# Cached pages loaded with two neighbouring tokens to a partition, in a hybrid decoder step on one Trainium2 core

## What is computed

```python
D_MODEL = 1024; SEQ = 512; DEC_BATCH = 8; DEC_SEQ = 4; PAST_LEN = 4096; PAGE_SIZE = 128
N_HEADS = 8; HEAD_DIM = 64; MOBA_BLOCK = 256; MOBA_TOPK = 3; D_FF = 4096

def moba_sample(q, k, v, cache_k, cache_v, layer, page_table, rel_bias):
    past = cache_k[layer, page_table[:, :own * ppb]]            # 32 pages of 128 tokens for each sequence
    kmean = jnp.mean(past.reshape(DB, own, MOBA_BLOCK, N_HEADS, HEAD_DIM), axis=2)
    gate = jnp.einsum('bhtd,bhnd->bhtn', qh, kmean)             # a score for each block of two pages
    _, sel = lax.top_k(gate, n_sel)                             # the three best blocks of 16
    ...
    return moba_attend(qh, qpos, rel_bias, k_own, v_own, kpos_own, sel_part)

def layer_out(x, attn, pool, mods, w_out, norm_mlp, w_up, w_down):
    x = x + g1 * (jnp.concatenate([attn, pool], axis=-1) @ w_out)
    h = rms_norm(x, norm_mlp) * (1 + sc2) + sh2
    return x + g2 * (jnp.square(jax.nn.relu(h @ w_up)) @ w_down)
```

## Time and profile before

| | us |
|---|---|
| three runs | 883.03, 884.61, 887.43 |
| median | 884.61 |
| the profiled execution | 884.93 |
| its span, first to last instruction | 883.1 |
| TensorE busy in the span | 836.8 (95%) |
| VectorE, ScalarE, GpSimd busy | 444.8, 336.5, 292.9 |
| DMA packets | 168097, 254.03 MB |
| share of the 16 DMA engines, SyncE's queue | 83.4% |

### The profile page before, as it was taken

One profiled execution on the slowest core, in us unless ns is written; L12 is line 12 of the kernel. 1 busy time (PEld: TensorE's weight loads), 2 busy tenths in 40 slices (PEclk: granted clock), 3 DMA queues, 4 the chain that ended last, 5 costly groups with the idle time before them and its releaser, 6 DMA issues.

```text
span 883.1 us, 20264 instructions
## 1 busy us (share of the span) xinstructions
PE 836.8 (95%) x7664; PEld 590.1 (67%) x7664; DVE 444.8 (50%) x850; ACT 336.5 (38%) x701; POOL 292.9 (33%) x191
## 2 busy tenths in 40 slices
PE   5899999998998799999999999999999999999985
PEld 3677777665776366666666666667667666578874
DVE  2743222764778784664674574575565450221222
ACT  4232222887012664337127127127127127123111
POOL 0330002957132263344244244244244244323200
PEclk9799999999999899999999999999999999999998
DMA  8942226698998679999999999999899989988997
GB/s 298 335 158 96 96 74 256 197 339 258 310 305 250 221 224 313 333 346 339 319 322 309 315 320 313 303 324 316 294 340 330 343 251 365 304 315 300 396 398 281
DMA packets 168097, 254.03 MB, mean 288 GB/s; under 512 B 10502, under 2 KB 69723, under 8 KB 168027
## 3 DMA queue, kind: packets, MB, share of 16 engines
q1 hardware_dynamic: 167267, 250.66, 83.4%
q0 software_dynamic: 768, 2.51, 0.7%
HBM read 248.56 MB, written 4.75 MB: 287 GB/s over the span
## 4 chain that ended last, share of the span: by engine, by line
PE 83%; DVE 6%; DMA 3%; ACT 3%; issue 2%; POOL 1%; SPq 1%; DVEq 0%; ACTq 0%
PE PS L1587 80%; POOL hT_split L656 1%; DMA W<-in_cache_v_dram 1%; DMA mixT<-in_x_prompt_dram 1%; PE PS L1936 1%; DMA W<-in_w_up_dram 1%; PE PS L1810 1%; DVE W L1356 1%; DVE mixT L1296 1%; DVE hT L1135 1%; ACT mixT L905 1%; DVE xT L1424 1%; PE PS L2166 1%; DVE mixT L1293 0%; DVE stat L1298 0%
## 5 line engine op out<-in xcount | busy, mean ns | idle before, releaser
L718 POOL TENSOR_TENSOR W_split<-W,W_split 128x1024 fp32r<-128x1024 f32 x72 | 172.4, 2394 | 311.7 <-ACT W_split L878 141.9
L1587 PE MATMUL PS<-gT_split,W_split 128*128 128x512 f32 x576 | 200.0, 407 | 1.0 <-DVE xT L1424 0.2
L1356 DVE STREAM_TRANSPOSE W<-rwT 128x512 f32<-128x512 f32 x256 | 163.4, 683 | 59.4 <-DMA rwT<-in_cache_k_dram 36.5
L1587 PE MATMUL PS<-rwT_split,W_split 128*128 128x512 f32 x512 | 178.0, 409 | 5.8 <-POOL hT_split L656 5.8
L1587 PE MATMUL PS<-hT_split,W_split 128*128 128x512 f32 x416 | 162.5, 400 | 0.5 <-ACT mixT L951 0.5
L1587 PEld LDWEIGHTS PS<-gT_split,W_split 128*128 128x128 f32 x576 | 108.5, 188 | 54.2 <-issue 18.0
L1587 PEld LDWEIGHTS PS<-rwT_split,W_split 128*128 128x128 f32 x512 | 97.4, 190 | 40.6 <-issue 16.6
L878 ACT ACTIVATE W_split<-W 128x1024 fp32r<-128x1024 f32 x32 | 33.9, 1059 | 178.8 <-DMA W<-in_w_up_dram 178.8
L1587 PE MATMUL PS<-kT_split,W_split 128*128 128x512 f32 x256 | 100.1, 391 | 0.6 <-issue 0.6
L1424 DVE SCALAR_TENSOR_TENSOR xT<-PS,mods,xT 128x512 f32<-128x512 f32 x64 | 47.2, 738 | 101.8 <-PE PS L1587 101.6
L1587 PEld LDWEIGHTS PS<-hT_split,W_split 128*128 128x128 f32 x416 | 79.5, 191 | 16.3 <-issue 1.6
(11 more groups left out here) (286 smaller groups left out, 956.8 us busy)
## 6 DMA issues: line engine op xcount, KB each, us to landing
W<-in_cache_v_dram SPq DMA_DIRECT2D x256, 256.0 KB, 4.0
rwT<-in_cache_k_dram SPq DMA_DIRECT2D x256, 256.0 KB, 4.2
W<-in_w_ada_dram SPq DMA_DIRECT2D x12, 2048.0 KB, 10.7
W<-in_w_up_dram SPq DMA_DIRECT2D x32, 512.0 KB, 5.7
W<-in_w_down_dram SPq DMA_DIRECT2D x32, 512.0 KB, 5.8
W<-in_w_down_dram SPq DMA_DIRECT2D x6, 2048.0 KB, 15.5
W<-in_w_in_dram SPq DMA_DIRECT2D x3, 2048.0 KB, 7.9
rwT<-in_w_up_dram SPq DMA_DIRECT2D x3, 2048.0 KB, 10.2
```

The costliest lines, as they stand in the source:

```text
L718: pool.tensor_tensor(rows_part(RAW, q, W_split), rows_part(RAW, q), rows_part(HIGH, q, W_split), ALU.subtract).then_inc(w_low, 1)
L1356: dve.transpose(ktb[u % 2][:, :, g, :], k_ring[:, j % SLOTS, pg, :]).then_inc(kt_ev, 1)
L1587: return pe.matmul(out, lhsT, rhs, start=start, stop=stop, **kw)
```

## The change

It has three parts.

1. A page's tokens go two by two onto 64 partitions: tokens 2r and 2r + 1 of a block's first page lie side by side on partition 2r, those of the second page on partition 2r + 1. The two ring places `pg` now hold the even and the odd tokens of both pages instead of one page each.
2. The order of keys within a block changes with it, so the bias table of the last page is spread over 64 columns, where each partition of the first page has the far bias. `C32["last"]` grows from 512 to 1024 columns, `const32` moves, four bias matmuls get 256 columns instead of 128, and `lastr` and the slices in `scores_out` follow.
3. On GpSimd `take_queries(i + 3)` moves from the head of `back` to the place ahead of `up_low(i + 1, 1)` in `front`.

```diff
-for _name, _n in (("ownmask", DB * NS), ("rev", REV + 1), ("far", P), ("last", DT * P), ("own", DT * NS), ("spread", P)):
+for _name, _n in (("last", DT * 2 * P), ("ownmask", DB * NS), ("spread", P), ("rev", REV + 1), ("far", P),
+                  ("own", DT * NS)):
...
     for t in range(DT):
-        for key in range(P):
-            c32[bucket(P + t - key), o + t * P + key] = 1.0
+        for p in range(P):
+            for side in range(PPB):
+                at = p // 32 * 64 + side * 32 + p % 32
+                key = p // PPB * PPB + side
+                c32[bucket(P + t - key) if p % PPB else 31, o + t * 2 * P + at] = 1.0
...
-        lastr = sb("lastr", [P, 32])
+        lastr = sb("lastr", [P, 64])
...
-        const32 = rw[0:32, 3072:3072 + C32_W]
+        const32 = rw[0:32, 2816:2816 + C32_W]
...
                 for pg in range(PPB):
-                    sp.dma_start(ring[:, slot, pg, :], cache[bass.ds(phys[pg], 1), :, :].rearrange("a p n -> (a p) n"))\
+                    sp.dma_start(ring[pg:P:PPB, slot, :, :],
+                                 cache[bass.ds(phys[pg], 1), :, :].rearrange("a (p s) n -> (a p) s n", s=PPB))\
                       .then_inc(landed[slot], 16)
...
-            def front(i, more=True):
+            def front(i, keys=False, more=True):
 
                 hidden_low(i, HP - 1)
                 down_low(i, 2)
                 down_low(i, 3)
                 if more:
                     up_low(i + 1, 0)
-                    up_low(i + 1, 1)
-
-            def back(i, keys=True):
-
                 if keys:
                     take_queries(i + 3)
+                if more:
+                    up_low(i + 1, 1)
+
+            def back(i):
+
                 up_low(i + 1, 2)
...
-                dve.tensor_tensor(near_last, bank(4, P, P, P).rearrange("p (g n) -> p g n", g=QUADS),
-                                  own_quad[:, :, None].to_broadcast([P, QUADS, 32]), ALU.mult).then_inc(last_raw, 1)
+                dve.tensor_tensor(near_last, bank(4, P, 2 * P, 2 * P).rearrange("p (g n) -> p g n", g=QUADS),
+                                  own_quad[:, :, None].to_broadcast([P, QUADS, 64]), ALU.mult).then_inc(last_raw, 1)
...
-                lo, mid, hi = 512 * half, 512 * half + (480 if half else 512), 512 * half + 512
+                lo, mid, hi = 512 * half, 512 * half + (448 if half else 512), 512 * half + 512
...
             for t in range(DT):
-                lo = C32["last"][0] + t * P
-                last = mm(bank(4, P, P, P), relrows[:, t, :], const32[:, lo:lo + P], t == 0, t == DT - 1)
+                lo = C32["last"][0] + t * 2 * P
+                last = mm(bank(4, P, 2 * P, 2 * P), relrows[:, t, :], const32[:, lo:lo + 2 * P], t == 0, t == DT - 1)
```

More of the change, by code:

```diff
@@ L256, in decoder_step @@
         relown = rw[0:32, 6912:6912 + DT * HT].rearrange("p (s h t) -> p s h t", s=DT, h=NH)
-        near_last = cmps[:, 0:P].rearrange("p (g n) -> p g n", g=QUADS)
+        near_last = cmps[:, 0:2 * P].rearrange("p (g n) -> p g n", g=QUADS)
         ada_sums = [rw[:, 7168:7168 + PIECE], rstd[:, :]]
@@ L778, in _ @@
             stream_low(h_hi, h2_high, h2_ready)
+            take_queries(2)
             back(-1)
             with pool.Fori(0, LAST - 2) as i:
-                front(i)
+                front(i, keys=True)
                 back(i)
             front(LAST - 2)
-            back(LAST - 2, keys=False)
+            back(LAST - 2)
             front(LAST - 1)
-            back(LAST - 1, keys=False)
+            back(LAST - 1)
             front(LAST, more=False)
```

## The result

The changed kernel takes 906.4 us (median of 904.21, 906.02, 906.79 and 912.31) where the kernel before took 883.8 beside it: a ratio of 1.0263, 95% interval 1.0202 to 1.0323. It is slower by 22.6 us, and 884 us was forecast. The profiled execution took 904.21 us, its span is 902.4.

What follows compares the result with a forecast made beforehand. The prediction took TensorE to bound the kernel, with DMA the runner-up. Pages at -1.9 us and bias matmuls at +1.1 gave -0.8, 883.8 against the median, called 884 us; range 876 to 893.

Steps and rivals of the forecast that it cites:

- the small edits: Constants' transfer, VectorE's wider columns, scores, GpSimd queries and SyncE's issues: all counted at nothing; +0.4 us if the transfer lacks cover.
- The pages' saving: Page transfers: a 4 KB packet replaces two of 2 KB, 16 ns or 9% less a pair; -1.9 us at the end.
- Place (ii): Near 740 to 773 us, the last batch's late value pages delay weighing matmuls by 2.0 us; 1.7 of it saved.
- Place (i): TensorE's 2.5 us wait for ScalarE, behind a w_up quarter queued after key pages; 0.25 us saved.
- The bias matmuls: In the opening, four matmuls of 256 columns instead of 128 add 1024 column passes: +1.1 us, bounds 1.1 to 2.1.
- The queries: On GpSimd, moved ahead of the second quarter's low part, which ends about 510.9 instead of 509.2, before TensorE's use: no cost.
- The shared write ports: Rival: pages on alternate partitions make engines share ports and packets slower; 959 us at 243 ns, 1083 at 324; chance 0.18.
- the 195: In the turns, the ns a 4 KB packet may take before pages no longer fit in a turn.
- No larger packets: Rival: the two tokens still go as 2 KB each, leaving only the bias matmuls: 886 us; chance 0.08.
- DMA is the bound after all: Rival: full DMA engines delay TensorE unseen; each turn gives back up to 4.1 us, total 860 us; chance 0.11.

Runs made afterwards that it cites:

- SyncE relieved everywhere: Changed kernel with one load of four page numbers instead of two loads of two, for all 256 blocks: 886.09 us, ratio 1.0005.
- neighbouring halves: Changed kernel with each page on 64 neighbouring partitions instead of every second one: median 1031.0 us; with four-number loads in the turns as well, median 1033.8 us.
- kernel without the pages: Changed kernel with the page transfers of the kernel before (128 packets of 2 KB); wider bias tables and moved queries stay: 885.56 us, ratio 1.0013.
- relieved kernels: Changed kernel with four-number page loads: in the turns 888.07 us, for all blocks 886.09; in the turns with pages written as 32 x 2 rows, 890.54.
- eight-shape probe: Kernel before with 24 transfers added at its start on SyncE, eight shapes three times: issues 465 to 492 ns for 64 rows, 312 to 352 for others.

## Why the prediction was wrong

**The step that failed** is the last sentence of the small edits: "SyncE issues as many transfers as before, in the same places", costed at nothing. The count and the places were right and the price was taken as unchanged. It is 142 ns more each, 9.1 us a turn, against 4.8 to 7.7 us of waits in the turns after the first, which one question to the trace of before would have shown. Even at an unknown price a bound was to be had: over 7.7 / 64 = 0.12 us an issue, SyncE becomes the bound. The prediction took DMA for the runner-up behind TensorE (0.94 of 66.8 us is 62.8); SyncE's queue, at 59 to 62, stood as near and was not added up.

**The pages' saving** was over-sized. The sum took 89 ns for a 2 KB packet and 162 for one of 4 KB, from two windows outside the turns. By the packets' times in the fourth turn, a 2 KB packet took 94 ns in the mean before and a 4 KB packet 189 in the changed kernel, 189 too with SyncE relieved everywhere: a pair saved nothing (by the medians, 2 x 84 and 159, 9 ns). The share of a turn is 0.91 to 0.92, not 0.88, and that fall is the longer turn: 0.939 x 66.7 = 62.6 us of each engine before, 0.911 x 69.5 = 63.3 after. Place (ii), the late value pages, was counted at -1.7 us and has the wrong sign: the late arrivals that add up to 2.0 us in the earlier trace rows add up to 3.7 in the changed kernel, where eight pages are issued in 7.62 us instead of 6.32, and to 2.8 with SyncE relieved everywhere. So the longer issue has a part in it; how much is a backlog of transfers, as the prediction read it, is not shown. Place (i) went from 2.5 us to 1.3, in one profile each; the kernels above, neighbouring halves left aside, have 0 to 3.4 there.

**The bias matmuls** were put at +1.1. The block of 22 rows with the projection behind it starts at 33.52 and the first projection matmul at 38.23: 4.71 us, and 4.87 before. The granted clock differed: 0.75 over that stretch, between the levels of 1.2 and 2.4 GHz, and 0.50 before. Other kernels have like clocks: with 128 columns the stretch took 4.27 us at 0.74 and 4.26 at 0.77, with 256 columns 4.68 to 4.77 at 0.73 to 0.75 (three kernels, the changed one among them); at 0.88 to 0.90 both took 4.27. So the added columns cost some 0.4 to 0.5 us at the lower of these clocks and nothing that can be seen at the higher, less than half of what was counted. All small parts together are the 1.0013 of the kernel without the pages, within the 0.5% that can be told. **The queries** cost nothing, as forecast.

**The rivals.** The shared write ports had the sign, but did not decide in this layout: 189 ns lies below the 195 from which they would (204 by the 14.5 us that the turn's other packets took instead of 17.0), and turns of 66.8 us with 4 KB pages and a relieved SyncE fit the argument against them (alternate partitions are spread over all 128). With neighbouring halves full engines came true, at 270 ns and 1006.9 us or more. "No larger packets" fell with the count. "DMA is the bound after all" fell with the relieved kernels: fewer packets, same turns. By the Trainium skill (Perfetto Trace Analysis, DMA Optimizations) larger rows pay off where the kernel is DMA-bound; these turns were not, so no run here tests that, but two 2 KB packets took no longer than one of 4 KB (188 against 189 ns). The queue that decided was in none of the rivals. The skill (DMA: Bandwidth & Descriptors, Issuing engines are not separate DMA queues) calls the time to initiate a DMA "usually small relative to the DMA itself". That is so here, 0.475 us against a median of 4.0 to land, and still SyncE bounds: its issues follow one another, while 64 page transfers of 4.0 us fit into a turn of 69.

## What to carry to other kernels

Add up the issuing engine's queue per turn as you add up TensorE's: issues, register loads and waits; its waits are the slack, and a new transfer shape has a new issue price. Before changing the layout of a transfer, time the issue of the new shape alone, as the eight-shape probe does, and if the issuing queue becomes the bound, take register loads off it (one load of four numbers took 298 ns, two loads of two took 948). When fewer packets bring a lower DMA share and a longer turn, look for the queue that feeds them.

## What was not expected of the hardware

- The issue of a transfer of 64 rows took 465 to 492 ns, of 32, 96 or 128 rows 0.31 to 0.35 us on an idle queue, whatever the row size (second and third time over; the first time up to 0.59 and 0.40); 64 rows written as two dimensions took 538 in the kernel.
- Reading page numbers into registers: 272 ns for one, 474 for two, 298 for four (medians; the last in the kernel with four everywhere).
- In the turns, 4 KB packets took 189 ns in the mean to every second partition and 270 to 64 neighbouring ones, and two 2 KB packets 188.
- A longer loop body on SyncE lost 3.4 to 5.9 us a turn where the loop turns back, with 40 instead of 19 instruction packets.
